# Two experts' products issued in turn, one in each half of the TensorE array

## What is computed

```
hb = silu(xb @ w_gate[e]) * (xb @ w_up[e])
y  = hb @ w_down[e]
```

## Time and profile before

| | us |
|---|---|
| median of 3 runs | 6293.67 (6289.52 to 6301.94) |
| span of the profiled execution | 6278.8 |
| median less that span | 14.9 |
| TensorE busy | 5120.2 |
| VectorE busy | 1663.1 |
| ScalarE busy | 891.7 |

### The profile page before, as it was taken

The page is one execution under the profiler, slowest core; times in us unless marked ns, Lnnn a source line. Parts: engine busy times, 40 slices in busy tenths (PEclk is TensorE's granted clock), DMA queues, the critical chain, the costliest instruction groups (busy, mean ns, idle before and its releaser), DMA issues. The chain is left out here.

```text
span 6278.8 us, 52914 instructions
## 1 busy us (share of the span) xinstructions
PE 5120.2 (82%) x20330; PEld 2500.9 (40%) x20330; DVE 1663.1 (26%) x3413; ACT 891.7 (14%) x1549; POOL 0.2 (0%) x4
## 2 busy tenths in 40 slices
PE   2587377776999997889879999965894678599998
PEld 2532366643333332334433333343443633333332
DVE  7812633422111111013221111113007610211111
ACT  0001111112111112122121111122102210200001
POOL 0000000000000000000000000000000000000000
PEclk9998788987999998875679999977897789799999
DMA  8620000003666650100046666521120021087774
GB/s 322 228 80 15 4 0 0 0 27 136 240 240 240 236 192 28 54 28 0 27 155 233 232 237 240 187 69 35 43 67 1 1 80 49 9 318 274 277 275 150
DMA packets 396549, 790.14 MB, mean 126 GB/s; under 512 B 19408, under 2 KB 104528, under 8 KB 396448
## 3 DMA queue, kind: packets, MB, share of 16 engines
q1 hardware_dynamic: 396448, 788.81, 35.3%
HBM read 786.68 MB, written 2.10 MB: 126 GB/s over the span
## 5 line engine op out<-in xcount | busy, mean ns | idle before, releaser
L1333 PE MATMUL ps<-arena 128*64 128x512 f32 x3072 | 1248.9, 594 | 4.3 <-ACT arena L1373 4.3
L335 PE MATMUL ps<-arena 128*128 128x512 f32 (+1 forms) x2560 | 1074.7, 583 | 184.0 <-DMA arena<-in_w_in 51.5
L335 PEld LDWEIGHTS ps<-arena 128*128 128x128 f32 x2560 | 501.1, 197 | 755.5 <-issue 566.6
L1333 PEld LDWEIGHTS ps<-arena 128*64 128x64 f32 x3072 | 398.7, 137 | 786.6 <-issue 786.6
L1362 PE MATMUL ps<-arena 128*64 128x512 f32 x1536 | 589.6, 595 | 6.2 <-ACT arena L1373 6.2
L1438 DVE TENSOR_TENSOR arena<-arena,ps 128x512 f32<-128x512 f32 x48 | 33.0, 687 | 1170.0 <-ACT arena L1389 1170.0
L1314 PE MATMUL ps<-arena 128*128 128x512 f32 x688 | 334.3, 618 | 7.2 <-ACT arena L1373 3.5
L1304 PE MATMUL ps<-arena 128*128 128x512 f32 x688 | 311.0, 606 | 30.7 <-DVE small L1426 30.7
L1362 PEld LDWEIGHTS ps<-arena 128*64 128x64 f32 x1536 | 188.4, 137 | 368.5 <-issue 368.5
L1373 ACT ACTIVATE arena<-ps 128x512 f32<-128x512 f32 x340 | 180.7, 599 | 1080.3 <-PE ps L1304 559.5
L1414 DVE TENSOR_SCALAR arena<-arena,small 128x64 f32<-128x64 f32 x344 | 59.9, 250 | 794.7 <-PE ps L1362 758.6
(11 more groups left out here) (337 smaller groups left out, 4693.2 us busy)
## 6 DMA issues: line engine op xcount, KB each, us to landing
arena<-in_moe_wgate SPq DMA_DIRECT2D x64, 2048.0 KB, 9.6
arena<-in_moe_wup SPq DMA_DIRECT2D x64, 2048.0 KB, 14.4
arena<-in_moe_wdown SPq DMA_DIRECT2D x64, 2048.0 KB, 8.4
arena<-in_w_e_gate SPq DMA_DIRECT2D x32, 2048.0 KB, 7.9
arena<-in_w_e_up SPq DMA_DIRECT2D x32, 2048.0 KB, 12.8
arena<-in_w_e_down SPq DMA_DIRECT2D x32, 2048.0 KB, 8.7
arena<-in_ada_w SPq DMA_DIRECT2D x24, 2048.0 KB, 12.3
arena<-in_w_in SPq DMA_DIRECT2D x36, 1024.0 KB, 7.7
```

The source lines that it names most:

```text
L335: mm = nc.tensor.matmul(K.ps[:, b * 4 + m, 0:tok], wb[b][:, k, m * P:(m + 1) * P], rhs[:, k, :], start=(k == 0), stop=(k == kt - 1))
L1333: last = mm(K.ps[half[b], j, :], xg[:, k, half[b]], W[b][j][:, k, :], start=(k == 0), stop=(k == KT - 1))
```

## The change

Within a pass, the loops are turned round. For each matrix (gate, then up; later down) the matmuls of A and B alternate: the first contraction step of A, the first of B, the second of A, and so on. TensorE waits for both experts' gate matrices, does all gate products, then waits for both up matrices, and so on; there is one signal when a matrix is done for both. SyncE follows: after the gate products it loads both gate matrices, after the up products both up matrices, after the down products both down matrices. ScalarE waits for the steps under their new names. No instruction of arithmetic is added or removed.

```diff
-                    for b, x in enumerate("AB"):
-                        sp.wait_ge(pe_s.sem, last(f"up{x}"))
-                        sp.dma_start(W[b][0], wg(i, b, c).rearrange("(k p) n -> p k n", p=P)).then_inc(w_in[b][0], 16)
-                        sp.dma_start(W[b][1], wu(i, b, c).rearrange("(k p) n -> p k n", p=P)).then_inc(w_in[b][1], 16)
-                    for b, x in enumerate("AB"):
-                        sp.wait_ge(pe_s.sem, last(f"down{x}"))
-                        sp.dma_start(down[b], wd(i, b, c).rearrange("(k p) n -> p k n", p=P)).then_inc(w_in[b][2], 16)
+                    for j, (name, src) in enumerate((("gate", wg), ("up", wu), ("down", wd))):
+                        sp.wait_ge(pe_s.sem, last(name))
+                        for b in range(2):
+                            dst = down[b] if name == "down" else W[b][j]
+                            sp.dma_start(dst, src(i, b, c).rearrange("(k p) n -> p k n", p=P)).then_inc(w_in[b][j], 16)
...
-                    for b, x in enumerate("AB"):
-                        for j in range(2):
+                    for j in range(2):
+                        for b in range(2):
                             pe.wait_ge(w_in[b][j], (i * H + c) * 16 + 16)
-                            pe.sem_inc(rounds, 1)
-                            for k in range(KT):
+                        pe.sem_inc(rounds, 1)
+                        for k in range(KT):
+                            for b in range(2):
                                 last = mm(K.ps[half[b], j, :], xg[:, k, half[b]], W[b][j][:, k, :], start=(k == 0), stop=(k == KT - 1))
                         last.then_inc(pe_s.sem, 1)
...
-                    for b, x in enumerate("AB"):
+                    for b in range(2):
                         pe.wait_ge(w_in[b][2], (i * H + c) * 16 + 16)
-                        pe.sem_inc(rounds, 1)
-                        for q in range(2):
-                            for k in range(FTL):
+                    pe.sem_inc(rounds, 1)
+                    for q in range(2):
+                        for k in range(FTL):
+                            for b in range(2):
                                 last = mm(K.ps[half[b], 4 + q, :], hidT[:, k, half[b]], down[b][:, k, q * 512:(q + 1) * 512],
                                           start=(c == k == 0), stop=(c == H - 1 and k == FTL - 1))
-                        last.then_inc(pe_s.sem, 1)
+                    last.then_inc(pe_s.sem, 1)
...
-                    act.wait_ge(pe_s.sem, pe_s.at(f"upB{c}", i))
+                    act.wait_ge(pe_s.sem, pe_s.at(f"up{c}", i))
...
-                act.wait_ge(pe_s.sem, pe_s.at(f"downB{H - 1}", i))
+                act.wait_ge(pe_s.sem, pe_s.at(f"down{H - 1}", i))
```

More of the change, by code:

```diff
@@ L1265, in experts @@
     for c in parts:
-        pe_names += [f"upA{c}", f"upB{c}"] + (backs if c == 0 else []) + (["gather"] if c == H - 1 else []) + [f"hid{c}"]
-        pe_names += (["gates", "x"] if c == H - 1 else []) + [f"downA{c}", f"downB{c}"]
+        pe_names += [f"gate{c}", f"up{c}"] + (backs if c == 0 else []) + (["gather"] if c == H - 1 else []) + [f"hid{c}"]
+        pe_names += (["gates", "x"] if c == H - 1 else []) + [f"down{c}"]
         act_names += [f"silu{c}"] + (["row0", "row1"] if c == H - 1 else []) + [f"hid{c}"]
```

## The result

The changed kernel takes 5585.58 us (median of 4 runs, 5575.89 to 5592.1) against 6291.6 us (4 runs of the kernel before, 6280.65 to 6301.94). The ratio is 0.8876, with a 95% interval of 0.886 to 0.8892: 706 us less. The prediction was 5585, in the range 5560 to 5690.

A forecast was written before the change was run, and what follows sets the result against it. TensorE was taken to bound the kernel, with the DMA becoming the second block's bound after the change. Savings of 495.8 + 213.5 = 709 us off 6278.8 give 5570, plus 14.9 makes 5585 us; range 5560 to 5690.

The forecast's parts named there:

- Full overlap: Expert passes: every matmul runs beside one of the other column half, 35.84 us becoming 20.22, saving 15.62 us a pass.
- B: Rival on the expert passes: overlap incomplete, slot 0.489 us or worse, total 5685 us; chance 0.16.
- C: Rival on the expert passes: weight loads laid bare stop both halves, total 5863 to 6178 us; chance 0.04.
- E: Rival on the expert passes: both halves writing one PSUM bank make the second wait, slower at 6529 us; chance 0.04.
- D: Rival on the second block: DMA slower than its queued rate, at 350 GB/s, total 5643 us; chance 0.11.
- The 14% of rows 6: Upper end for the slot, from L1998 and L2000: 14% over full overlap, slot 0.489, 2.9 us a pass.
- The first block's stages: First block, two stages of 16 pairs: 247.9 us saved a stage, 495.8 for both, with 8.4 at each start.
- No wait for the DMA in steady passes of the first block: First block: loads take 32.3 us of a 37.75 us pass at 390 GB/s, with margins above 9 us.
- The second block bound by the DMA: Second block, 16 passes: DMA becomes the bound at 390 GB/s, 32.3 us a pass, saving 213.5 us.
- the main line of the forecast: Second block's clock: gaps before the up products leave it at 1.00; a fall would cost 18 us.
- The sum: Whole kernel: 495.8 + 213.5 = 709 us off the profiled span of 6278.8 us, giving 5570.
- The 14.9 us beside the span: Whole kernel: median of runs 6293.67 us lies 14.9 above the profiled span; kept, bringing 5570 to 5585 us.

The follow-up runs named there:

- e5_one_half: Changed kernel with both experts' products sent through array columns 0-63, the second expert's into other PSUM banks: 6529.48 us, ratio 1.0384 to the kernel before.
- e1_by_matrix: Changed kernel, but inside each matrix all products of one expert stand before all of the other (8 and 8 matmuls): 6139.13 us, ratio 0.9762 to the kernel before.
- e6_half_down: Changed kernel, but in the second block only half the rows of each down matrix are loaded: 5554.2 us, ratio 0.8833 to the kernel before.
- e8_early_signal: Changed kernel with TensorE's signal that gate and up buffers are free moved ahead of its wait for VectorE's tables: 5560.67 us, ratio 0.8844 to the kernel before.

## Why the prediction was right, step by step

- **Full overlap** (the 15.62 us a pass): measured 53.37 - 37.76 = 15.61. The reading of rows 3 and 5 carried it, and e5_one_half and e1_by_matrix show that the two column halves are its cause, not the alternation or the waits. Rivals B, C and E fall with the pairs of loads every 0.43 us, and D with the 394 GB/s of the second block. The 14% of rows 6 does not carry over; what costs it there was not tested.
- **The first block's stages.** From the first gather record to the end of the last down a stage took 869.1 us before and takes 2143.81 - 1518.55 = 625.3: 243.9 saved, 247.9 forecast. The missing 4 us lie in the first pass: from the gather's first record to that of the give back it took 39.35 us before and 34.73 after, 4.6 saved where I had 8.4. Two terms were off. I let the up products start when 8.4 MB had passed at the queue's rate, 23.9 us after the gather's start (1530.4 - 1506.53); they start at 26.0. By the windows 8.3 MB had passed at 1542.6 (369 GB/s since 1520) and 9.1 MB at 1544.5 (373 GB/s), when they start. The first down loads had been issued by then (1530.75), so some of those bytes may be theirs, or the signal may come later than the bytes; the runs don't tell the two apart. And I let them run at the steady pace; behind the wait they take 8.78 us, 1.7 more. The gate products are 1.7 us longer as well, but that hides in the wait for the up matrices. I had looked at the clock for the second block's gaps only. I also misread the start of the loads: the issue at 1507.94 is the third of SyncE's weight loads, the first is at 1506.65. It did no harm, since the term was worked out from the bytes up to 1510.
- **No wait for the DMA in steady passes of the first block**: right, no load is waited for there and TensorE is busy 37.27 of 37.76 us.
- **The second block bound by the DMA**: right, at 394 GB/s and 31.9 us a pass, where I had 390 and 32.3; e6_half_down shows the bound. From the first gather record on the stage took 744.4 us before and takes 5546.25 - 5018.43 = 527.8: 216.6 saved, 213.5 forecast. The idle time before the up products is 1.56 to 1.86 us, where I had 2.3, and the clock stays at 1.00 behind it, as in the main line of the forecast.
- **The sum**: 243.9 + 244.2 (second layer, by the same two points) + 216.6 = 704.7 us against 709 forecast; the medians differ by 706.
- **The 14.9 us beside the span** were a wrong reading that did no harm. A run's time is 1.8 us above its span (5592.1 and 5590.3); the rest was that the profiled run of the kernel before, 6280.65 us, was its fastest, and the profiled run of the changed one its slowest. The spans differ by only 688.5 us. The 16 us between lie outside the expert stages, 7.3 of them in the recurrence of the first block, which the change doesn't touch; the other 9 were not followed. The windows over it, before and after:

```profile
715.53:1281.30 565.77, 436.13 (x6807) 0.88 0.00 0
```

```profile
717.69:1290.80 573.11, 443.55 (x6808) 0.87 0.00 0
```

The same work, at a granted clock of 0.88 and 0.87; why the clock differs is open. Adding the difference back gave the right number all the same, since it only took the forecast from the fast run to the median. That the total came within 1 us owes something to errors of opposite sign: 4 us too many for each stage of the first block, 3 too few for that of the second, and medians that vary by more than what is left.

## What to carry to other kernels

When two products use different column halves of the array, as here in float32 with 512 moving elements, look in the timeline for the place where one follows the other: if both lines start at full pace for a few records, issuing them in turn, alternately or in groups of two matmuls, makes that last, and a group of four already loses part. Before counting the gain, divide the bytes of a pass by the queued rate of the DMA, since that is the next bound, and look at the first pass by itself. At a stage's start, follow the first load back to the signal that lets it go; here one line in the wrong place held the expert loads for 8.6 us in the first stage (from the load of the seat numbers to the first weight load it is 9.31 us in the changed kernel and 0.70 in e8_early_signal).

## What the runs showed of the hardware

- Records of one column half start beside the other half's up to 3.9 records deep: the same figure from four orders with 3 to 11 changes of half a pass. With groups of two matmuls (four records) nothing is lost, with four matmuls 5.4 of 48.
- It makes no difference that both halves write the same PSUM bank at once: e1_by_matrix's five changes, two of them within a bank, come to 3.9 each, and the changed kernel reaches 48 of 48.
- The pace of 0.43 us a record holds for each half while the other runs and while the DMA moves 394 GB/s: in the second block 32 records still take 7.04 to 7.09 us.
- A wait of 3.01 us and one of 2.05 us at a stage's start were each followed by a fall to half clock within a microsecond (0.50 in 1534.6 to 1535.0 and in 1544.7 to 1545.0), while waits of 1.56 and 1.86 us in the steady passes were not (1.00). Before the wait of 2.05 us TensorE had run 8.78 us of products, in part at half clock; before those of 1.56 and 1.86 us some 7 us of them at full clock.
